# Each expert's rows added straight into the outputs by its scatter, gates applied to the activations

## What is computed

```python
logits = (h @ router_w) + router_b
top_vals, top_idx = lax.top_k(logits, 4)          # 32 experts, 4 for each token
gates = jax.nn.softmax(top_vals, axis=-1)
...
gu = xb @ w_gate_up[e] + b_gate_up[e]             # 1024 -> 2 x 1024
g = jnp.minimum(gu[:, :D_FF], 7.0)
u = jnp.clip(gu[:, D_FF:], -7.0, 7.0)
act = (u + 1) * g * jax.nn.sigmoid(1.702 * g)
return act @ w_down[e] + b_down[e]                # 1024 -> 1024
...
y[token] = x[token] + sum over its 4 experts of gate * expert_row
```

## Time and profile before

| | us |
|---|---|
| median of 3 runs (1729.86 to 1739.68) | 1736.56 |
| the profiled execution, its own time | 1735.41 |
| its span, first to last instruction | 1733.7 |
| expert loop, from the first gather to the last scatter's issue | 652.7 to 1696.4 |
| from there to the end | 37.3 |

### The profile page before, as it was taken

The page is one execution under the profiler, slowest core; times in us unless marked ns, Lnnn a source line. Parts: engine busy times, 40 slices in busy tenths (PEclk is TensorE's granted clock), DMA queues, the critical chain, the costliest instruction groups (busy, mean ns, idle before and its releaser), DMA issues.

```text
span 1733.7 us, 32093 instructions
## 1 busy us (share of the span) xinstructions
PE 1474.0 (85%) x11950; PEld 595.0 (34%) x11951; DVE 782.4 (45%) x1160; ACT 356.0 (21%) x822; POOL 96.7 (6%) x173
## 2 busy tenths in 40 slices
PE   3868887779788978899998998999899999899970
PEld 2433333346433354332332332333233332232320
DVE  2789879997786335221332232132132131131326
ACT  3212212222222111111211211212112122121220
POOL 0000010000000000000100000000000000000000
PEclk8989995679898857999999999999899999999995
DMA  9557888988998785598999999999999999999986
GB/s 327 182 187 258 283 295 272 331 279 292 311 301 270 242 352 207 227 392 339 429 420 403 427 417 396 412 418 411 392 421 412 401 428 411 397 428 399 428 351 253
DMA packets 127292, 598.10 MB, mean 345 GB/s; under 512 B 20503, under 2 KB 20517, under 8 KB 102026
## 3 DMA queue, kind: packets, MB, share of 16 engines
q1 hardware_dynamic: 109088, 560.20, 81.9%
q10 hardware_dynamic: 8634, 20.00, 3.4%
q0 software_dynamic: 9504, 17.06, 2.6%
HBM read 589.36 MB, written 25.87 MB: 355 GB/s over the span
## 4 chain that ended last, share of the span: by engine, by line
PE 40%; DMA 19%; DVE 2%; issue 1%; ACT 0%; DVEq 0%; SPq 0%; ACTq 0%
PE bank L1511 25%; DMA wts<-in_w_gate_up 16%; PE bank L1548 8%; PE bank L1530 4%; DMA wts<-in_w_down 3%; PE bank L1501 1%; PE bank L1618 1%; DVE v_ring L2139 1%; PE bank L1559 1%; PE bank L1599 0%; DVE q_b L2139 0%; DMA h_tok<-h_rows,v_tok 0%; ACT k_T L1155 0%; DVEq L2127 0%; ACT k_T L1138 0%
## 5 line engine op out<-in xcount | busy, mean ns | idle before, releaser
L1511 PE MATMUL bank<-wts,h_T 128*32 128x512 f32 x4032 | 443.9, 597 | 9.7 <-DMA wts<-in_w_gate_up 5.2
L2061 DVE TENSOR_SCALAR q_T<-bank 128x512 f32<-128x512 f32 x32 | 22.1, 692 | 636.9 <-PE bank L1511 636.9
L1511 PEld LDWEIGHTS bank<-wts,h_T 128*32 128x32 f32 x4032 | 129.5, 111 | 308.3 <-issue 296.4
L1548 PE MATMUL bank<-wts,k_T 128*32 128x512 f32 x2048 | 228.3, 597 | 8.0 <-issue 4.9
L1530 PE MATMUL bank<-wts,h_T 128*32 128x512 f32 x992 | 132.6, 675 | 52.2 <-DMA wts<-in_w_gate_up 50.4
L1658 DVE TENSOR_TENSOR wts<-wts,q_b 128x1024 f32<-128x1024 f32 x128 | 158.1, 1235 | 23.1 <-DMA wts<-in_cache_k 17.4
L1661 DVE TENSOR_REDUCE sc<-wts 128x16 f32<-128x1024 f32 x128 | 156.2, 1220 | 4.4
L1145 ACT ACTIVATE h_T<-bank 128x512 f32<-128x512 f32 x66 | 35.9, 595 | 573.5 <-PE bank L1501 573.5
L1548 PEld LDWEIGHTS bank<-wts,k_T 128*32 128x32 f32 x2048 | 64.9, 110 | 149.0 <-issue 139.5
L1223 PE MATMUL bank<-wts,h_T 128*8 128x128 f32 (+1 forms) x480 | 92.7, 465 | 12.3 <-ACT h_T L854 6.4
L1155 ACT ACTIVATE k_T<-bank 32x256 f32<-32x256 f32 x256 | 95.7, 374 | 13.6 <-PE bank L1548 10.2
(11 more groups left out here) (330 smaller groups left out, 1375.8 us busy)
## 6 DMA issues: line engine op xcount, KB each, us to landing
wts<-in_w_gate_up SPq DMA_DIRECT2D x126, 2048.0 KB, 15.8
wts<-in_w_down SPq DMA_DIRECT2D x64, 2048.0 KB, 18.3
wts<-in_cache_k SPq DMA_DIRECT2D x256, 256.0 KB, 3.7
v_ring<-in_cache_v SPq DMA_DIRECT2D x160, 256.0 KB, 3.8
wts<-in_cache_v SPq DMA_DIRECT2D x96, 256.0 KB, 3.9
wts<-in_w_in SPq DMA_DIRECT2D x5, 2048.0 KB, 24.1
wts<-y_rows SPq DMA_DIRECT2D x4, 2048.0 KB, 15.1
wts<-in_w_out ACTq DMA_DIRECT2D x8, 512.0 KB, 6.2
```

The costliest lines, as they stand in the source:

```text
L1511: m = nc.tensor.matmul(PS[part][p0:p0 + 32, :], lhs[:, 32 * b:32 * b + 32], rhs[:, part * F + half * 512:part * F + half * 512 + 512], sta ...
L1548: m = nc.tensor.matmul(PS[4][p0:p0 + 32, :], act_T[0][:, k, a0:a0 + 32], chunk[c][:, k, n * 512:(n + 1) * 512], start=(c == 0 and k == 0), ...
```

## The change

The gates move in front of the down product: since the expert's output is linear in the activations, a row's gate can be multiplied into its activations. The output then needs only an addition, and the indirect transfer itself does it (`compute_op=ALU.add`: the row in HBM is read, added to, and written).

- `x2` rows are stored straight into the outputs `y_prompt` and `y_sample` (`part_r` on ScalarE); scatter 0 waits for these stores. `x2_rows` is not used, nor read back.
- `scatter` issues two indirect transfers for each expert: one into `y_prompt`, with the pair number shifted right by 2 as row, and one into `y_sample`, with that exclusive-or 512. Each drops the rows that are out of its bounds. `y_scattered` counts 32 for each expert.
- The tables carry a gate beside each pair number: the products of `part_r` and of `enter_late` get twice the columns, and `spread` puts the gates where the two halves of the activations have their rows. `select` reads one more index and copies the expert's two gate columns into `gcol`; the last multiplication of each half becomes one with a column factor.
- The read of `y_rows`, the 20 weighted additions and the five stores at the end are gone.

```diff
-        slots = v_tok[:, 1, 0:TCOLS].bitcast(i32)
-        slot_tok = v_tok[:, 1, 64:64 + TCOLS].bitcast(i32)
+        slot_row = v_tok[:, 1, 0:2 * TCOLS].bitcast(i32).rearrange("p (c a) -> p c a", a=2)
...
# SyncE
-            sp.wait_ge(x2_out, 16 * (TILES + 1))
-            sp.wait_ge(late_slots_done, 1)
-            for u, s in enumerate(TAIL):
-                sp.dma_start(out_acc[u][0:rows_of(s), :], x2_rows[row0[s]:row0[s] + rows_of(s), :]
-                             ).then_inc(x2_back, 16)
...
-            sp.wait_ge(y_scattered, (n + E) * 16)
-            sp.wait_ge(w_used[5], n + E)
-            for u in OUT_ORDER:
-                r, m = row0[TAIL[u]], rows_of(TAIL[u])
-                sp.dma_start(out_rows[u][0:m, :],
-                             y_rows[r * TOPK:(r + m) * TOPK, :].rearrange("(p k) n -> p (k n)", k=TOPK)
-                             ).then_inc(y_loaded[u], 16)
-            sp.wait_ge(y_stored, 16 * (TILES + 1))
# GpSimd, scatter
-                    pool.wait_ge(y_scattered, i * 16)
-                V.link(nc.gpsimd.tensor_copy(y_idx, slots[:, bass.ds(column(i, first), 1)]))
-                pool.reg_add(bound, rows_0, PAIRS - 1)
-                pool.indirect_dma_start(y_rows[:, :], bass.IndirectOffsetOnAxis(y_idx, 0), y_sb, None,
-                                        bounds_check=bound, oob_is_err=False).then_inc(y_scattered, 16)
+                    pool.wait_ge(y_scattered, i * 32)
+                V.link(nc.gpsimd.tensor_copy(y_idx, slot_row[:, bass.ds(column(i, first), 1), :]))
+                for a, (rows, n_rows) in enumerate(((y_prompt[0], SEQ), (y_sample[:, 0, :], NB))):
+                    pool.reg_add(bound, rows_0, n_rows - 1)
+                    pool.indirect_dma_start(rows, bass.IndirectOffsetOnAxis(y_idx[:, a:a + 1], 0), y_sb, None,
+                                            bounds_check=bound, oob_is_err=False, compute_op=ALU.add
+                                            ).then_inc(y_scattered, 16)
...
+            pool.wait_ge(x2_out, 16 * (TILES + 1))
             scatter(0, True)
...
+            pool.wait_ge(y_scattered, (n + E) * 32)
# ScalarE
-                act.dma_start(x2_rows[r:r + n, :], x2[0:n, :]).then_inc(x2_out, 16)
+                act.dma_start(y_out[s], x2[0:n, :]).then_inc(x2_out, 16)
...
-            for no, u in enumerate(OUT_ORDER):
-                act.wait_ge(pair_done, TOPK * (no + 1))
-                act.dma_start(y_out[TAIL[u]], out_acc[u][0:rows_of(TAIL[u]), :]).then_inc(y_stored, 16)
# TensorE
-                    m = nc.tensor.matmul(M[:, 0:E], at_rank[0:n, k, :], id_of[0:n, k, :], start=(k == 0),
+                    m = nc.tensor.matmul(M[:, 0:2 * E], at_rank[0:n, k, :], id_gate[0:n, k], start=(k == 0),
# VectorE
+            def spread(cols, gate):
+                for p0 in range(0, P, 64):
+                    nc.vector.tensor_copy(gate_tab[p0:p0 + 64, 0, cols], gate[0:64, :])
+                for q in range(4):
+                    s0 = 64 + 32 * (q // 2)
+                    last = nc.vector.tensor_copy(gate_tab[32 * q:32 * q + 32, 1, cols], gate[s0:s0 + 32, :])
+                V.link(last)
             def select(i):
                 e = dve.value_load(e_tab[0:1, bass.ds(i, 1)], min_val=0, max_val=E - 1)
+                c = dve.value_load(col_tab[0:1, bass.ds(i, 1)], min_val=0, max_val=TCOLS - 1)
+                V.link(nc.vector.tensor_copy(gcol.unsqueeze(2), gate_tab[:, :, bass.ds(c, 1)]))
...
+            V.link(nc.vector.tensor_scalar(slot_row[:, 0:E, 1], slots, 2, SEQ, ALU.logical_shift_right,
+                                           ALU.bitwise_xor))
+            spread(slice(0, E), slot_gate)
             select(0)
...
-                    mul(act_tok[part], u_act[part], s_act[part]).then_inc(act_done, 1)
+                    nc.vector.scalar_tensor_tensor(act_tok[part], u_act[part], gcol[:, part:part + 1], s_act[part],
+                                                   ALU.mult, ALU.mult).then_inc(act_done, 1)
...
-            for no, u in enumerate(OUT_ORDER):
-                m, acc = rows_of(TAIL[u]), out_acc[u]
-                dve.wait_ge(y_loaded[u], 16)
-                for k in range(TOPK):
-                    nc.vector.scalar_tensor_tensor(acc[0:m, :], out_rows[u][0:m, k * D:(k + 1) * D],
-                                                   gates[0:m, u, k:k + 1], acc[0:m, :], ALU.mult, ALU.add
-                                                   ).then_inc(pair_done, 1)
```

More of the change, by code:

```diff
@@ L349, in hybrid_step @@
         bias_hi, bias_rest = [sem(n) for n in ("bias_hi", "bias_rest")]
-        y_stored, x2_back, gu_done = [sem(n) for n in ("y_stored", "x2_back", "gu_done")]
+        gu_done = sem("gu_done")
         ids_done, entry_done, entry_summed, slot_part = [sem(n) for n in (
@@ L376, in hybrid_step @@
         (taps_done, fold_done, mask_done) = [sem(n) for n in ("taps_done", "fold_done", "mask_done")]
-        (counts_done, late_entered, late_summed, meta_out, bias_in, gathered, y_scattered, pair_done) = [sem(n) for n in (
-             "counts_done", "late_entered", "late_summed", "meta_out", "bias_in", "gathered", "y_scattered",
-             "pair_done")]
+        (counts_done, late_entered, late_summed, meta_out, bias_in, gathered, y_scattered) = [sem(n) for n in (
+             "counts_done", "late_entered", "late_summed", "meta_out", "bias_in", "gathered", "y_scattered")]
         (xt_full, xt_copied, gclip_done, sig_done, act_done, at_full, at_copied, y_front, y_back,
@@ L731, in gather @@
                 pool.wait_ge(slots_done, 1)
-                V.link(nc.gpsimd.tensor_copy(g_idx, slot_tok[:, bass.ds(column(i, first), 1)]))
+                V.link(nc.gpsimd.tensor_copy(g_idx, slot_row[:, bass.ds(column(i, first), 1), 0]))
                 pool.reg_add(bound, rows_0, TOK - 1)
@@ L1151, in copy_y @@
                 if not first:
-                    act.wait_ge(y_scattered, i * 16)
+                    act.wait_ge(y_scattered, i * 32)
                 for b in range(2):
@@ L1896, in part_r @@
                 V.link(total(chosen[0:n, u, :], onehot[0:n, u, :, :].rearrange("p k e -> p e k")))
-                V.link(mul(gtmp[0:n, :, :], onehot[0:n, u, :, :],
+                after(dve, slot_part, u)
+                V.link(mul(id_gate[0:n, :, 1, :], onehot[0:n, u, :, :],
                            gates[0:n, u, :].unsqueeze(2).to_broadcast([n, TOPK, E])))
-                total(gsum[0:n, :], gtmp[0:n, :, :].rearrange("p k e -> p e k")).then_inc(gate_done, 1)
+                total(gsum[0:n, :], id_gate[0:n, :, 1, :].rearrange("p k e -> p e k")).then_inc(gate_done, 1)
                 yield
@@ L2081, in copy_y @@
                 if not first:
-                    dve.wait_ge(y_scattered, i * 16)
+                    dve.wait_ge(y_scattered, i * 32)
                 V.link(nc.vector.tensor_copy(y_sb[0:64, 0:512], PS[4][0:64, :]))
@@ L2106, in late_tables @@
                 V.link(nc.vector.tensor_scalar(late_free, late_free, 0.0, float(UNUSED), ALU.max, ALU.min))
-                V.link(nc.vector.tensor_copy(slots[:, E:], late_free))
-                nc.vector.tensor_scalar(slot_tok[:, E:], slots[:, E:], 2, None, ALU.logical_shift_right
+                V.link(nc.vector.tensor_copy(slots[:, 0:LATE], late_free))
+                V.link(nc.vector.tensor_scalar(slot_row[:, E:, 1], slots[:, 0:LATE], 2, SEQ, ALU.logical_shift_right,
+                                               ALU.bitwise_xor))
+                spread(slice(E, TCOLS), late_gate)
+                nc.vector.tensor_scalar(slot_row[:, E:, 0], slots[:, 0:LATE], 2, None, ALU.logical_shift_right
                                         ).then_inc(late_slots_done, 1)
```

55 lines of the change are left out of this document (28 added, 27 removed).

## The result

| | before | after |
|---|---|---|
| median, us | 1732.16 (1729.86 to 1739.68, 7 runs) | 1744.07 (1743.06 to 1745.45, 7 runs) |
| ratio, 95% interval | | 1.0062 [1.0045, 1.008] |
| span of the profiled execution | 1733.7 | 1742.2 |
| expert loop, first gather to last scatter's first issue | 652.7 to 1696.4 | 650.0 to 1728.6 |
| from there to the end of the span | 37.3 | 13.7 |

The end became 23.6 us shorter and the loop 34.9 us longer; it began 2.8 us earlier. That is +8.5 us of span between these two executions. Forecast were -31.3 and +16.5.

What follows compares the result with a forecast made beforehand. The prediction took DMA to limit the expert loop, with one hole for each pair. Span 1733.7 - 31.3 + 16 + 0 + 0.5 = 1718.9 us, 1722 on the median; 8-in-10 range 1703 to 1750.

Steps and rivals of the forecast that it cites:

- Term 2: Expert loop: the addition in memory reads each scattered row before writing it; +16 us, between 0 and 39.
- rival 2: Expert loop: the scatters' load is uneven and counts whole, 39 us; 1745, or 1765 in a worse form; chance 0.20.
- the hole: Once per pair of experts: DMA share 0.70 over 6 us, 1.8 us idle, said to absorb large experts' added rows.
- Term 1: End of the kernel: 37.3 us after the last scatter's issue removed, 6.0 us in its place; -31.3 us.
- 10 or more would break term 1: Sign at the end: 6 us expected from the last scatter's first issue to the span's end; 10 or more refutes.
- Term 3: Expert loop, waits through the longer scatter: 0 us, as long as it lands within 22.9 us; 18.1 us estimated.
- rival 3: Expert loop: the scatter becomes a wait for copies and TensorE; at 40 us, 105 us more, 1827; chance 0.10.
- Term 4: VectorE: longer `select`, some 1.2 us for each expert, and some 3 us in front of expert 0; +0.5 us counted.
- the share of 0.98 in the long stretch: Expert loop: uneven load counting whole should put the mean DMA share in a pair's long stretch under 0.98.
- the forecast: Whole kernel: median 1722 us, band 1710 to 1730, faster than before; chance 0.55.
- Rival 1: Expert loop: the addition's read is free, overlapped or taken by the holes; 1706 us; chance 0.15.

Runs made afterwards that it cites:

- k1_plain: The changed kernel with the addition taken out of its two scatters, plain writes instead: 1713.6 us, ratio 0.99 to before.
- k2: The changed kernel with the adding scatter into the prompt's output alone, the sample rows' transfer dropped: 1741.8 us, ratio 1.006 to before.
- k8: The changed kernel with plain scatters, the prompt rows written a second time into an unused buffer: 1742.2 us, ratio 1.0042 to before.
- k4: The kernel before without its end (read of `y_rows`, additions, stores), nothing in their place: 1707.4 us, ratio 0.986 to before.
- k3: The changed kernel with the last wait for the scatters on SyncE instead of GpSimd, and a VectorE mark of landing: 1742.7 us, ratio 1.0069 to before.
- k9: The changed kernel with prompt scatters and all gathers in halves of 64 places, empty passes skipped, a GpSimd landing mark: 1740.9 us, ratio 1.0042 to before.
- k6: The changed kernel with the loop over 16 empty further blocks put under one condition: 1741.7 us, ratio 1.0045 to before.
- k11: The kernel before with its plain scatter in two halves of 64 places, gathers whole: 1719.5 us, ratio 0.9927 to before.
- k5_halves: The changed kernel with the prompt rows' adding scatter in two transfers of 64 places each: 1716.9 us, ratio 0.9902 to before.

## Why the prediction was wrong

**Term 2, the step that failed.** It put +16 us on the addition; 34.2 were measured (k1_plain to after). The pieces it was built from held: no row out of bounds costs anything to speak of (k2: 2 us), the read counts like a transfer (k8), and a scatter costs by the eight rows of its fullest engine and not by all its rows: 34.2 / 32 = 1.07 us, against the 1.22 that rival 2 used. The lay-out was misread (50 rows lie on eight engines, with four to eight each, and not on seven with eight), but the fullest has eight rows either way. Over 252 such rows, 167 ns more for each (327 less 160) are 42 us, of which 34.2 reached the loop. Two choices failed. The middle was taken between even and uneven for the small experts (14.5 of 8.5 to 20.8), though the landing times spoke for uneven alone (the 29-row scatter, whose fullest engine has four rows, is the one that moved its rows in half the time). And the large experts' scatters were put into the hole, at 1.5 us instead of up to 18.3. The hole is mean idleness and not room: the share over it stayed 0.70. In its middle just half of the engines were busy, in before and then in after:

```profile
1125.00:1126.00 1.00, 1.00 (x16) 0.39 (x12) 0.00 (x0) 0.00 (x0) 0.00 (x0) 1.00 0.50 213
1126.00:1127.00 1.00, 1.00 (x16) 0.26 (x8) 0.00 (x0) 0.00 (x0) 0.00 (x0) 1.00 0.50 213
```

```profile
1135.00:1136.00 1.00, 1.00 (x16) 0.39 (x12) 0.00 (x0) 0.00 (x0) 0.00 (x0) 1.00 0.50 168
1136.00:1137.00 1.00, 1.00 (x16) 0.26 (x8) 0.00 (x0) 0.00 (x0) 0.00 (x0) 1.00 0.53 201
```

In after the rows of the large expert's scatter (1125.02) move until 1136.5, and SyncE issues the next chunks at 1136.25. That the busy half is the one that carries the scatter follows from the lay-out above, not from a record. How much of the 34.2 us the large experts have was not measured by itself. A mean over 16 engines can't show that one of them is late.

The sentence of the Trainium skill that the prediction quoted (Collectives: The Full Stack, "The bandwidth ceiling: the fold count and why AG ≠ RS ≠ AR"), that a reducing transfer is slower for its two source reads, is borne out here with a size: an added 4 KB row is as dear as writing it twice, 34.2 against 36.8 us of the loop.

**Term 1** put -31.3 us; the span gave -23.6, k4's medians -25.0. The landing was sized right, 6.0 us against 6.3 (k3) and 6.2 (k9). What was left out is all that follows it, some 7 us: about 2 of empty passes (13.7 to 11.8 in k6's profile), and 4 to 5.5 that stay unexplained. The criterion "10 or more would break term 1" was met.

**Term 3** (no wait on the scatter) held: no row of after has ScalarE, VectorE or GpSimd waiting for a scatter. Only four quarters brought that wait about, and rival 3 at most that far. **Term 4**, +0.5 us, is too small to be seen beside the rest.

**The rivals.** Rival 2 came true, in its mild form: forecast 1745, measured 1744.07. Its price was 5 us too high (39 for 34) and its end 8 us too short. That the sum meets the median is in part luck: it stood on a median of before of 1736.6, from three runs, where seven gave 1732.16. Against before it said +8.2 us, and +11.9 were measured. The prediction held the share of 0.98 in the long stretch of before against it. Yet plain transfers lay as unevenly there (k11 gained 14 us by spreading them), and doubling their load moved the mean share by 0.01 to 0.02 only (over 1100 to 1500 us 0.98 in before, 0.97 in after, 0.96 in k8): a loss of 2% of the loop's 1040 us is 21 us, so a share of 0.98 in place of 1.00 was no evidence against it but some for it. Rival 2 had 0.20 and the forecast 0.55, and the reason was only that a middle looked safer than an end. Rival 1 (free) is excluded by k1.

**The best version** here is k5_halves, 1716.9, 27 us below after. Beside k11 (1719.5, the kernel before with the same repair) it can't be told apart: the intervals of their ratios overlap. So once the rows are spread, no gain of moving the sums into the transfers is clear of the noise (3 us by the medians), and the placement was worth 14 us in the one kernel and 27 in the other.

## What to carry to other kernels

Where the DMA queue is the limit, price an indirect transfer by its fullest engine, whole, not by its bytes over sixteen: a list of 128 places that is filled up to the middle loads half of the engines, and every large transfer waits for them. If two bounds differ only in whether the load is even, take the one that a row supports, not the middle, and don't put work into a hole in the mean share unless you know whose hole it is. An addition in memory is two writes of the row; it pays only where what it replaces costs more, and splitting the scatter's list in two is the first thing to try (not the gather's, which lost by it here). Count the fullest engine's rows before splitting further: here four pieces left it what two did.

## What the runs showed of the hardware beside this

- An adding indirect transfer keeps GpSimd for 1.57 us (128 places) or 1.43 (64), a plain one of the same form for 1.02 and 0.91: with four adding quarters (1.32 each) GpSimd is busy 300 us of the span.
- Gathers of 64 places slowed the weight traffic by some 4% for each byte over 400 us (92.9% of the engines' time for 151.5 MB against 92.6% for 157.0), at a share of 1.00, all of it while their rows moved. Unexplained, seen in two kernels.
- Behind a last indirect scatter the program ran on for 4.0 us (k9, empty passes skipped) to 7.0 us (k3) after everything had landed.
- The first 64 places of an indirect list of 128 lay on eight engines, four neighbouring ones of every 32 on each; in lists of 64 and of 32, two of every 32 lay on each of sixteen. A 4 KB row took its engine 160 ns plain and 327 ns adding.
